# Sparse attention's scores over all 128 rows, and a later second output weight

## The reference, cut to what matters

```python
def block(args):                       # 128 queries at a time, 4 such blocks
    logits = einsum('bqhd,bsd->bqhs', qib, ki)             # indexer, 8 heads of 64
    score = einsum('bqhs,bqh->bqs', relu(logits), wib)     # + causal mask
    _, idx = lax.top_k(score, 128)
    ks, vs = k[idx], v[idx]                                # 2 key/value heads of 64
    s = einsum('bqgrd,bqkgd->bqgrk', qg, ks) * scale       # 8 query heads, 4 for each key head
    p = softmax(s)
    o = einsum('bqgrk,bqkgd->bqgrd', p, vs)
```

## Time and profile before

| | |
|---|---|
| median of 3 runs | 3558.42 us (3556.67 to 3565.21) |
| the profiled execution's own time | 3563.61 us |
| its span | 3561.8 us (1.8 us lie around it) |
| PE busy | 3378.9 us, 95% of the span |
| DVE, ACT, POOL busy | 54%, 39%, 12% |
| mean granted TensorE clock | 0.963 of 2.4 GHz |

### The profile page before, as it was taken

How to read it: one execution, slowest core, us unless ns; L and a number is a source line. 1 busy time by engine, 2 the same in 40 slices (tenths; PEclk the granted TensorE clock), 3 DMA queues, 4 the chain that set the end, 5 groups by cost and what they waited for, 6 DMA issues and landing times. The chain is left out here.

```text
span 3561.8 us, 43151 instructions
## 1 busy us (share of the span) xinstructions
PE 3378.9 (95%) x17900; PEld 2760.9 (78%) x17900; DVE 1920.5 (54%) x2892; ACT 1380.3 (39%) x1924; POOL 432.2 (12%) x217
## 2 busy tenths in 40 slices
PE   8999998999999999999999989999999998699995
PEld 6888787877888888887788878888777675588884
DVE  4434366884543444343658864434245433599985
ACT  3222345543322232123455543212344423377772
POOL 1000242000100010001430001000231000122222
PEclk9999999997999999999999999999999988699997
DMA  4443220001222222222200012222321111599993
GB/s 177 142 142 119 82 95 1 1 25 60 85 97 108 97 89 89 107 86 92 76 32 1 1 72 84 94 103 89 110 80 37 72 60 64 226 403 409 407 408 136
DMA packets 65986, 414.61 MB, mean 116 GB/s; under 512 B 6912, under 2 KB 11136, under 8 KB 22272
## 3 DMA queue, kind: packets, MB, share of 16 engines
q1 hardware_dynamic: 63488, 403.46, 30.4%
q0 software_dynamic: 2304, 8.39, 0.6%
HBM read 375.13 MB, written 36.70 MB: 116 GB/s over the span
## 5 line engine op out<-in xcount | busy, mean ns | idle before, releaser
L344 DVE TENSOR_TENSOR w_lo<-ring,w_hi 128x2048 fp32r<-128x2048 f32 x146 | 334.6, 2292 | 869.6 <-ACT w_hi L340 869.5
L340 ACT ACTIVATE w_hi<-ring 128x2048 fp32r<-128x2048 f32 x146 | 280.3, 1920 | 1000.7 <-PE bank L469 584.6
L469 PE MATMUL bank<-x_hi,w_lo 128*128 128x512 f32 x1344 | 533.5, 397 | 0.0
L469 PE MATMUL bank<-x_hi,w_hi 128*128 128x512 f32 x1344 | 527.3, 392 | 0.0
L469 PE MATMUL bank<-x_lo,w_hi 128*128 128x512 f32 x1344 | 524.2, 390 | 0.0
L469 PEld LDWEIGHTS bank<-x_lo,w_hi 128*128 128x128 f32 x1344 | 252.3, 188 | 62.2
L469 PEld LDWEIGHTS bank<-x_hi,w_lo 128*128 128x128 f32 x1344 | 252.3, 188 | 58.0
L469 PEld LDWEIGHTS bank<-x_hi,w_hi 128*128 128x128 f32 x1344 | 252.3, 188 | 54.4
L513 PE MATMUL bank<-h_hi,w_hi 128*128 128x512 f32 x704 | 274.0, 389 | 0.0
L513 PE MATMUL bank<-h_hi,w_lo 128*128 128x512 f32 x704 | 274.0, 389 | 0.0
L513 PE MATMUL bank<-h_lo,w_hi 128*128 128x512 f32 x704 | 273.8, 389 | 0.0
(11 more groups left out here) (566 smaller groups left out, 6793.9 us busy)
## 6 DMA issues: line engine op xcount, KB each, us to landing
ring<-slots SPq DMA_DIRECT2D x238, 1024.0 KB, 4.8
arena<-slots SPq DMA_DIRECT2D x92, 1024.0 KB, 8.2
x_rows<-v_first SPq DMA_DIRECT2D x23, 512.0 KB, 6.7
xn<-x_rows SPq DMA_DIRECT2D x23, 512.0 KB, 7.9
y_rows<-xn SPq DMA_DIRECT2D x23, 512.0 KB, 8.5
x_aside<-xT SPq DMA_DIRECT2D x3, 2048.0 KB, 6.3
xT<-x_aside SPq DMA_DIRECT2D x3, 2048.0 KB, 7.9
xT<-x_t SPq DMA_DIRECT2D x2, 1024.0 KB, 10.2
```

Of the source, the lines that this page charges most:

```text
L340: e.activation(w_hi[:, k % 2, :], ring[:, k % RING, :], ACT.Copy).then_inc(*act.step(("hi", k)))
L344: e.tensor_tensor(w_lo[:, k % 2, :], ring[:, k % RING, :], w_hi[:, k % 2, :].bitcast(F32), ALU.subtract).then_inc(*dve.step(("slot", k)))
L469: made = e.matmul(bank[b + f][:, :], w.rearrange("p (k n) -> p k n", k=KC)[:, c, f * P:(f + 1) * P], (x_hi, x_lo)[part][:, c, :], start=c ...
```

## The change

The keys of each head get a home of their own with 128 rows: the 64 rows of the other head are zero. Head group 0 uses block 4 of `S.turned`, with partitions 64 to 127 set to zero; head group 1 uses columns 512 to 1023 of one home of `ring`, with partitions 0 to 63 zero. POOL writes the zeros (two memsets of 64 x 512 after its last rotation), and PE waits for them before the first score. ACT copies the transposed keys of each token tile with two small copies (64 x 128) and the rest of that group with one copy of 3 blocks. A score then multiplies all 128 rows of a query block, with both heads in it, by one key home.

That home of `ring` is the one that the second output weight goes to. So SP waits for the last score before it issues that load, both engines split it after the 8 chunks (`ahead = 1`) and not in the sparse attention strand, and the delta rule's room in `ring` is laid out by the home's number (`late_slot`).

```diff
--- before.py
+++ after.py
@@ -302,6 +302,8 @@
                         e.dma_start(x_aside, xT).then_inc(x_saved, 16)
                     if k == OUT_AT[l]:
                         e.wait_ge(*pe.at("TLT", ("delta", l), 6, NT - 1))
+                    if k == OUT_AT[l] + 1:
+                        e.wait_ge(*pe.at("scores", ("dsa", l), 8 * NT - 1))
                     if k == OUT_AT[l] + RING:
                         e.wait_ge(*pe.at("state", l, NT - 1, 1))
                         e.wait_ge(*pe.at("delta_state", l, NT - 1, 1))
@@ -1489,8 +1491,10 @@
             R.vb = flat(R.v_).rearrange("p (t n) -> p t n", t=NT)
             projected = flat(xn)
             R.Xt, R.Tt = (quad(projected[:, n * 2048:(n + 1) * 2048]) for n in range(2))
-            R.Lt, R.T = (ring[:, 0, n * 1024:(n + 1) * 1024].rearrange("p (q h t) -> p q h t", q=2, h=4) for n in range(2))
-            R.att = heads4(ring[:, 1, 0:512])
+            late = late_slot(l)
+            R.Lt, R.T = (ring[:, 1 - late, n * 1024:(n + 1) * 1024].rearrange("p (q h t) -> p q h t", q=2, h=4)
+                         for n in range(2))
+            R.att = heads4(ring[:, late, 0:512])
             R.dec, R.low = (heads4(w) for w in R.W)
             R.state = S.late[:, 1536:1664].rearrange("p (c i) -> p c i", c=2)
             R.rest, R.vn, R.vs = (S.late[:, 1664 + n * 256:1920 + n * 256].rearrange("p (h i) -> p h i", h=4)
@@ -1823,6 +1827,9 @@
 
 
 
+        def late_slot(l):
+            return (OUT_AT[l] + 1) % RING
+
         def attention_room(l, A):
             S = Room()
             S.l = l
@@ -1845,6 +1852,7 @@
             S.o3 = S.other.rearrange("p (h d) -> p h d", d=HD)
             S.score, S.spare = over_tok.take(512), over_tok.take(512)
             S.positive, S.keeps = ([over_tok.take(512) for _ in range(2)] for _ in range(2))
+            S.keys_of = S.turned[:, 4, :], ring[:, late_slot(l), 512:1024]
             S.best, S.thr, S.need = col2[:, 64:72], col2[:, 71:72], col2[:, 72:73]
             S.attend = softmax_room(("dsa", l), over_tok, bank[5:8], 0, act)
             assert over_tok.at <= A.at
@@ -1971,7 +1979,7 @@
             for h in range(8):
                 part = half_of(h // 4)
                 blocks.append(Block(
-                    w, [(S.turned[part, h % 4, q * P:(q + 1) * P], S.turned[part, 4, 0:w])],
+                    w, [(S.turned[:, h % 4, q * P:(q + 1) * P], S.keys_of[h // 4][:, 0:w])],
                     S.keeps[q % 2][:, 0:w], lambda s: S.v[:, s, :], part, mixed[part, h % 4, q * P:(q + 1) * P]))
             return blocks
 
@@ -1991,6 +1999,7 @@
                     made.then_inc(*pe.step(("rotated", l, t, g)))
                     yield
             e.wait_ge(*act.at("rotated", l, NT - 1, 2))
+            e.wait_ge(*pool.at("other_half_zero", l))
             for q in range(NT):
                 w = P * (q + 1)
                 if q > 0:
@@ -2032,12 +2041,16 @@
                 yield
             for t in range(NT):
                 yield
-                for g in range(3):
-                    n = 4 if g < 2 else 2
+                ts = slice(t * P, (t + 1) * P)
+                for g, (first, n) in enumerate(((0, 4), (1, 3), (0, 2))):
                     e.wait_ge(*pe.at("rotated", l, t, g))
-                    e.activation(S.turned[:, 4 * g:4 * g + n, t * P:(t + 1) * P],
-                                 bank[5 + g][:, 0:n * P].rearrange("p (b t) -> p b t", b=n), ACT.Copy).then_inc(
-                        *act.step(("rotated", l, t, g)))
+                    if g == 1:
+                        for half in range(2):
+                            e.activation(S.keys_of[half][half_of(half), ts], bank[6][half_of(half), 0:P],
+                                         ACT.Copy).then_inc(*act.step())
+                    e.activation(S.turned[:, 4 * g + first:4 * g + first + n, ts],
+                                 bank[5 + g][:, first * P:(first + n) * P].rearrange("p (b t) -> p b t", b=n),
+                                 ACT.Copy).then_inc(*act.step(("rotated", l, t, g)))
                     yield
             for q in range(NT):
                 w = P * (q + 1)
@@ -2058,8 +2071,8 @@
                 yield from attention_act(e, S.attend, dsa_blocks(S, q), 8 * q, HD ** -0.5)
             e.wait_ge(*dve.at("rwkv_out", l))
             e.wait_ge(*pe.at("TLT", ("delta", l), 6, NT - 1))
+            split_act(e, OUT_AT[l])
             for n in range(2):
-                split_act(e, OUT_AT[l] + n)
                 yield
 
         def dsa_pool(e, S):
@@ -2076,6 +2089,9 @@
                     *pool.step())
                 e.tensor_tensor(w3[:, :, 32:64], S.heads[:, t, :, 0:32], sweep(sin[:, 32:64], 20), ALU.mult).then_inc(
                     *pool.step(("sines", l, t)))
+            for n, home in enumerate(S.keys_of):
+                own(e, pool)
+                e.memset(home[half_of(1 - n), :], 0.0).then_inc(*pool.step(*([("other_half_zero", l)] if n else [])))
 
         def dsa_dve(e, S):
             l = S.l
@@ -2161,8 +2177,8 @@
                 own(e, dve)
                 yield
                 yield from attention_dve(e, S.attend, dsa_blocks(S, q), 8 * q, HD ** -0.5)
+            split_dve(e, OUT_AT[l])
             for n in range(2):
-                split_dve(e, OUT_AT[l] + n)
                 yield
 
         def strands_pool(e, R, D_, S, N):
@@ -3277,7 +3293,7 @@
                                  "s": dsa_act(e, S[l])})
                 out_act(e, ("out", l), OUT_AT[l], 4, FFN_AT[l, 1], {
                     0: [act.at("out", ("dsa", l), 8 * NT - 1), pe.at("delta_y", l, NT - 1, 1)],
-                    6: [dve.at("delta_out", l)]}, 2)
+                    6: [dve.at("delta_out", l)]}, 1)
                 rows_act_in(e, (l, 1), par1("ffn_norm1"), [
                     [dve.at("res", ("out", l), 0, c)] + ([pe.at("down", (("out", l), 0), 7)] if c >= 6 else [])
                     for c in range(KC)])
@@ -3313,7 +3329,7 @@
                 e.wait_ge(const_landed, 16)
                 in_turns(TURNS, {"p": projections_dve(e, l, R[l], N[l]), "r": rwkv_dve(e, R[l]), "d": delta_dve(e, D_[l]),
                                  "s": dsa_dve(e, S[l])})
-                out_dve(e, ("out", l), OUT_AT[l], 4, FFN_AT[l, 1], OUT_ORDER, 2, (l, 1), par1("ffn_norm1"),
+                out_dve(e, ("out", l), OUT_AT[l], 4, FFN_AT[l, 1], OUT_ORDER, 1, (l, 1), par1("ffn_norm1"),
                         (x_back, 16 * (l + 1)))
                 if l + 1 < DEPTH:
                     ffn_dve(e, (l, 1), FFN_AT[l + 1, 0], (l + 1, 0), par1("ffn_norm0"))
```

## The result

The changed kernel took **3538.7 us** (median of 4 runs, 3536.9 to 3539.9), beside 3561.8 us (4 runs, 3556.7 to 3567.8) for the kernel before: a ratio of 0.9935 with an interval of 0.9918 to 0.9952, that is 23 us or 0.65% less. The profiled execution took 3539.92 us, with a span of 3538.1 and a mean clock of 0.968; before they were 3563.61, 3561.8 and 0.963, so the two profiles differ by 23.7 us where the medians differ by 23.1. The forecast was 3547 us within 3539 to 3560. The direction was right, the size was too small, and the result lies 0.3 us outside the range.

A forecast was written before the change was run, and what follows sets the result against it. PE, busy 95% of the span, was taken as the bound, with ACT nearly full in the first query block. Two layers of 4.0 us plus 8.8 us of clock, off 3563.6, gave 3547 us, range 3539 to 3560.

The forecast's parts named there:

- the price of a half-row score among full-array work: PE around 384-wide scores: 0.41 us for going in and coming out, 0.2 us for each change of shape.
- I take 1.5: First query block: 1.5 us a layer gained of 3.2 us PE time, as ACT leaves 2 us at most.
- I take 0.3: Second query block: 0.3 us a layer gained of 1.2 us PE time, since DVE works beside it.
- the 0.4 of lost overlap: Four scores a layer interleaved with half-row work in the array's other half: padding loses 0.4 us a layer.
- the far end of 14: Upper end of the two layers' gain without the clock term, put at 8.0 us with ends 0 and 14.
- I expect the long stretch to shrink to about a third: Layer 0's last stretch at low clock: 8.8 of 13.2 us gained under full-row scores; ends nothing and all 13.2.
- My case's own range: Whole kernel: the main forecast, with 62% chance, lies within 3538 to 3555 us.
- The clock does not care: Rival, 15%: rows do not raise the low clock, busy time is the same or less; whole kernel 3556 us.
- PE's saving is hidden: Rival, 12%: ACT and DVE set the pace, nothing gained on PE's path; 3556 us, or up to 3560.
- Lost concurrency: Rival, 4%: all 11 scores with a half-row neighbour lose their overlap, 6.7 us a layer; 3568 us.
- Slower: Rival, 7%: small shifts make layer 1's clock fall after its wait too, costing 13.2 us; 3573 us.
- the signs given: If right: 128-row scores, 0.88 us behind them, 705 to 730 us shorter by 2, last stretches 50 to 57 and 50 to 52.

The follow-up runs named there:

- run 5: Changed kernel with one product of 64 rows and one column ahead of every score, scores still full rows: 3568.9 us, 1.0006 against the kernel before.
- Run 6: Changed kernel with the indexer's products padded to full rows as well, its keys in two more homes with zeros: 3547.8 us, 0.9948 against the kernel before.
- the last block alone: Changed kernel with full-row scores in the fourth query block only, half rows in the first three: 3551.0 us, 0.9968 against the kernel before.
- run 4: Kernel before with only the later load and split of the second output weight added: 3562.0 us, 0.9987 against the kernel before.
- run 1: Changed kernel with 64-row scores again, keeping key homes, zeros, copies and later weight: 3563.4 us, 1.0003 against the kernel before.
- run 12: Changed kernel with full-row scores in the first three query blocks only, repeated on another chip: 3552.4 us, 0.9958 against the kernel before.

## Why the prediction was wrong in size

**Right: the price of a half-row score among full-array work.** Forecast 0.41 us, measured 0.39 in the rows above; half of it is in the score's own two records and not in its neighbours, as the working had it too, though it opens with "a score alone costs PE the same". In run 5 the entry to the small product and the exit from it cost 0.10 each. The Trainium skill's page "TensorEngine Tiling (Array Packing)" (Key Properties) says that changing the tiling mode drains the engine, without a price; the rows fit that and put 0.1 to 0.2 us on it.

**Wrong: the first block's low clock was put at nothing.** The prediction gave the clock to layer 0's last stretch alone. For the first block it had PE's saving only, "I take 1.5" of 3.2 us a layer, because ACT's 10.01 of 12 us left 2 at most. Measured were 3.1 and 3.3 us. From the first score's start to the sixth's, at full clock in both kernels, there is part of it: 593.80 - 586.04 = 7.76 us before, 593.72 - 586.74 = 6.98 after, 0.8 us, and only then PE waits for ACT:

```profile
593.72 0.39 PE L1889 MATMUL bank<-ring,arena 128*128 128x128 f32 x2
594.63 0.33 PE L1898 MATMUL bank<-const,arena 128*128 128x128 f32 x1 [0.52 <-ACT arena L1948]
```

So ACT does pace that part, as I said. Most of the rest is clock. Before, 595 to 602 us ran at 0.53 with PE busy for 6.64 of 7; after, all of 586 to 602 is at 1.00:

```profile
595.00:602.00 7.00, 6.64 (x29) 5.70 (x29) 2.68 (x15) 4.61 (x20) 0.00 (x0) 0.53 0.01 2
...
586.00:602.00 16.00, 12.41 (x90) 10.45 (x90) 8.14 (x43) 13.34 (x51) 0.00 (x0) 1.00 0.00 1
```

The work behind the last score, up to the indexer, has no score in it. Before, then after:

```profile
597.95 0.47 PE L1890 MATMUL bank<-const,arena 128*128 128x128 f32 x1 [0.30 <-ACT arena L1940]
...
603.26 3.88 PE L2003 MATMUL bank<-arena 64*128 64x256 f32 x16 [0.36 <-ACT mixed L1966]
...
597.41 0.33 PE L1898 MATMUL bank<-const,arena 128*128 128x128 f32 x1 [0.78 <-ACT arena L1948]
...
600.85 3.88 PE L2012 MATMUL bank<-arena 64*128 64x256 f32 x16 [0.36 <-ACT mixed L1974]
```

It took 603.26 - 597.95 = 5.31 us before and 600.85 - 597.41 = 3.44 after: 1.9 us of clock. In layer 1 it is 5.67 and 3.44, 2.2 us. Together that is 4.1 us that no term of the sum held. I had read the mean of 0.89 in the earlier trace rows and passed over it, because it was one short stretch and I was looking at the long one.

**Nearly right: the rest of PE's saving.** In the second block, "I take 0.3" of 1.2 was low: the whole came through, less the 0.4 of lost overlap, 0.8 us in both layers. The third block gave 2.25 and 1.9 for the forecast 2.0. The last gave 34.07 - 32.67 = 1.4 for 1.0. Over both layers the four blocks, with the last at full clock, gave 14.9 us, less 1.0 for the start: 13.9. Without the 4.1 of clock that is 9.8 where the forecast had 8.0. That 13.9 comes so near the far end of 14 is luck, since that end was made of changes of shape alone.

**Wrong: how much of the long stretch goes.** The step was "I expect the long stretch to shrink to about a third", 8.8 us. In layer 0 it went whole, 13.3 us; layer 1 got a short one of 7 us, 2.8 us dear. Together 10.4 us, and 13.9 + 10.4 = 24.3, of which the rest of the kernel takes 0.7 back. Of the 7.5 us above the forecast 16.8, then, 4.1 are the first block's clock, 1.8 the rest of PE's saving and 1.6 this term. The "third" had no row behind it: the full-row work after 870 us in the earlier trace rows, back in 2 of 5 us, would have said 2 us, and 7 were measured in layer 1.

**Wrong: the range.** The text carried 14 and 13.2 as far ends; together they give 3563.6 - 14 - 13.2 = 3536.4, and the range stopped at 3539. My case's own range, 3538 to 3555, held the result; the final one was cut at 3539. The two terms were taken as independent, and both held time at low clock: 4.1 us of the one and all of the other.

**The rivals.** *The clock does not care* (3556) fell: the last block alone was worth 0.32%, 11 us, of which its shapes pay 1.4 us a layer, and the first block's stretch is in 8 of 8 layers with half rows and in 0 of 18 with full ones. *PE's saving is hidden* (3556) fell by the blocks' lengths. *Lost concurrency* fell for the scores. The pair of the earlier trace rows took 1.08 us and now takes 639.46 - 638.27 = 1.19, for the 1.18 of the working:

```profile
638.27 0.60 PE L1889 MATMUL bank<-ring,arena 128*128 128x256 f32 x2
...
639.46 0.44 PE L1898 MATMUL bank<-const,arena 128*128 128x128 f32 x2
```

Run 6 shows that mechanism alive in the indexer. (The 3568 us of this rival also left out the clock's 8.8 without saying so; with them it would have been 3559.) *Slower* named a real thing: layer 1 did pay for a fall that it had escaped, but 2.8 us and not 13.2. The rule of the Trainium skill's page "TensorE: Matmul & The Clock Gate" (Part 1), that the clock follows how busy the engine has been, doesn't account for what ran here: 30.77 busy us of 31 stayed at the low level.

**What came as said.** L1889 has 128 rows only, eight records behind a score take 0.89 us, and the third block is 2 us shorter. The later weight is worth nothing (run 4); DVE's second split starts at 852.12 us with no wait ahead of it, and last score to reload is 11.86 us as before. POOL's zeros are two memsets of 0.52 us, done at 574.5, 12 us ahead of the first score at 586.74 (the bound was 1.54 each):

```profile
573.38 0.52 POOL L2094 MEMSET arena<- 64x512 f32 x1
573.96 0.52 POOL L2094 MEMSET ring<- 64x512 f32 x1
```

The last tile's copies cost 0.5 us a layer (forecast 0.45), and the first score waits 2.82 us for them where it waited 2.53. Of the signs given, layer 0's last stretch (51.55, said 50 to 57) came; layer 1's (54.49, said 50 to 52) did not.

**What stays open.** What makes the clock stay low. Half rows without shape changes were not run, and the small product adds a load and a short wait of its own to each score. The runs show that the change as a whole takes the first block's low stretch away, and that half-row products bring it back there whatever the scores' rows. For the last block they show the long stretch in 0 of 10 layers with full rows, in 4 of 12 with half rows and in 2 of 6 with the small products; these are few, the 10 are in part the same kernel again, and they don't say how the share falls between rows and changes. Nor do they say why run 1, with half rows, had its low stretch in another block.

## What to carry to other kernels

Price a narrow matmul together with its neighbours, start to start: of the 0.39 us that a half-row score cost here, half was in its own records and half in those around it. Pad a half-row product with zeros where it stands alone among full-array work, and leave it narrow where its neighbours use the other half (padding the scores gave 23 us; with the indexer padded as well, 9 of them were lost). And look at the spread of a kernel's runs before a forecast of tenths of a per cent: where a mean clock in a busy stretch is below 1, each such stretch is a term of its own, and terms with one cause can reach their ends together.

## What the runs showed of the hardware that I had not expected

- The clock stayed at its low level for 31 us with PE busy for 30.77 of them; in the profiled last blocks it did so four times with half rows (three times 31 us and once 21), and twice for some 24 us with full-row scores among small half-row products. One stretch of 31 us costs 13.3 us of time.
- In the first block a low stretch of 7 to 10 us stood 9 to 14 us behind the first score in all 10 profiled layers with half-row products at the scores, and in none of 18 without.
- The same kernel's time is stepped by it: three groups 12 to 13 us apart in run 12. The kernel before spreads over 16 us or more wherever it ran 13 times or more (3555.6 to 3572.2, 3557.5 to 3573.7, 3556.8 to 3578.9), the changed one over 3.3 in four runs. A change of shapes can be worth as much in spread as in its median.
- A product of 64 rows and a single column costs 0.31 us between full-array work, and 0.51 us with what it costs on either side.
- Half-row fp32 products in opposite halves overlap at width 512 (2.76 us for four, 3.53 padded). At width 256 eight of them took 3.80 us, and padded 3.73: there was nothing to lose. The eight of the changed kernel:

```profile
600.85 3.88 PE L2012 MATMUL bank<-arena 64*128 64x256 f32 x16 [0.36 <-ACT mixed L1974]
604.65 0.55 PE L870 MATMUL bank<-const,arena 128*128 128x128 f32 x3
```
